# Fetching each expert buffer of the last six turns in two bounded halves, the second from a reversed copy of the table

## The reference

```python
s = jnp.einsum('thpd,hpkd->thpk', q, sub_keys)
sv, si = lax.top_k(s, PEER_TOPK)
cidx = (si[:, :, 0, :, None] * N_KEYS + si[:, :, 1, None, :]).reshape(PEER_BLOCK, PEER_HEADS, -1)
best, pos = lax.top_k(cand, PEER_TOPK)
eidx = jnp.take_along_axis(cidx, pos, axis=-1)
g = jax.nn.softmax(best, axis=-1)
act = jax.nn.gelu(jnp.einsum('thkd,td->thk', expert_u[eidx], xb))
return jnp.einsum('thk,thkd->td', g * act, expert_v[eidx])
```

## Time and profile before

| | us |
|---|---|
| median of 3 runs (1407.13 to 1409.46) | 1408.75 |
| the profiled execution's own time | 1413.65 |
| its span, first to last instruction | 1412.3 |
| POOL busy in the span | 296.5 |
| turn 10's first fetch is issued at | 1138.81 |

### The profile page before, as it was taken

One profiled execution on the slowest core, in us unless ns is written; L12 is line 12 of the kernel. 1 busy time (PEld: TensorE's weight loads), 2 busy tenths in 40 slices (PEclk: granted clock), 3 DMA queues, 4 the chain that ended last, 5 costly groups with the idle time before them and its releaser, 6 DMA issues.

```text
span 1412.3 us, 17514 instructions
## 1 busy us (share of the span) xinstructions
PE 1034.5 (73%) x6217; PEld 599.6 (42%) x6217; DVE 887.4 (63%) x2281; ACT 477.8 (34%) x1313; POOL 296.5 (21%) x265
## 2 busy tenths in 40 slices
PE   7998999999899999988878777754544454434444
PEld 4776655577665646434553432332222222202200
DVE  6488633448863536643347779586867776877664
ACT  2013523101353411455236655433323222332312
POOL 0000000000000000000023255533645444443441
PEclk9998999999899899998879899886666766656665
DMA  7452452445346142153059899999999999999997
GB/s 297 152 194 103 182 220 84 171 165 181 121 188 242 55 155 97 34 227 136 1 231 395 341 419 426 426 426 423 412 426 427 426 426 426 427 426 425 426 426 312
DMA packets 56105, 391.12 MB, mean 277 GB/s; under 512 B 9931, under 2 KB 13054, under 8 KB 15954
## 3 DMA queue, kind: packets, MB, share of 16 engines
q0 software_dynamic: 37440, 268.45, 45.5%
q1 hardware_dynamic: 18578, 121.56, 23.2%
HBM read 387.89 MB, written 1.05 MB: 275 GB/s over the span
## 4 chain that ended last, share of the span: by engine, by line
DVE 18%; PE 16%; DMA 14%; ACT 6%; issue 3%; another core or an unknown queue 3%; POOL 2%; ACTq 0%; DVEq 0%
PE bank L169 15%; DMA e_uv<-in_experts_dram,e_listed 14%; DVE e_uv L2791 6%; POOL e_uv L2988 2%; ACT e_diag L230 1%; ACT L230 1%; DVE e_hot L185 1%; DVE e_rest L2722 1%; ACT m_W L230 1%; PE bank L174 1%; DVE e_si L2720 1%; DVE e_si L2726 1%; DVE e_e L210 0%; DVE e_sv L2718 0%
## 5 line engine op out<-in xcount | busy, mean ns | idle before, releaser
L2988 POOL DMA_INDIRECT e_uv<-in_experts_dram,e_listed x252 | 286.8, 1138 | 1080.3 <-DVE e_listed L202 839.6
L169 PE MATMUL bank<-e_uv,e_diag 128*32 128x512 f32 x1024 | 231.3, 885 | 283.4 <-ACT e_diag L230 275.5
L2791 DVE CUSTOM_DVE_ANT_0 e_uv<-e_uv,e_h2q 128x1024 f32<-128x1024 f32 x192 | 229.4, 1224 | 83.1 <-DMA e_uv<-in_experts_dram,e_listed 79.0
L169 PEld LDWEIGHTS bank<-e_uv,e_diag 128*32 128x32 f32 x1024 | 41.3, 140 | 410.2 <-ACT e_diag L230 316.6
L169 PE MATMUL bank<-hT,weights 128*128 128x256 f32 x640 | 145.4, 388 | 2.4 <-DVE hT L191 1.4
L169 PEld LDWEIGHTS bank<-hT,weights 128*128 128x128 f32 x640 | 123.9, 195 | 21.8 <-DVE hT L191 1.6
L230 ACT ACT_TABLE_LOAD x81 | 103.9, 1283 | 7.9 <-PE bank L169 1.9
L169 PE MATMUL bank<-weights,hT 128*128 128x512 f32 (+1 forms) x256 | 101.5, 552 | 1.5 <-DVE hT L191 1.5
L197 DVE SCALAR_TENSOR_TENSOR conv<-ubuf,vec,conv 128x256 f32<-128x256 f32 x240 | 96.8, 479 | 0.6
L230 ACT ACTIVATE e_act<-e_dot 128x4 f32<-128x4 f32 (+1 forms) x81 | 16.6, 205 | 234.6 <-DVE e_dot L2791 212.4
L169 PE MATMUL bank<-weights,mixT 128*128 128x512 f32 x192 | 88.6, 616 | 2.3 <-DVE mixT L202 1.6
(11 more groups left out here) (383 smaller groups left out, 1419.0 us busy)
## 6 DMA issues: line engine op xcount, KB each, us to landing
weights<-in_ada_dram SPq DMA_DIRECT2D x8, 2048.0 KB, 8.3
weights<-in_layer_out_dram SPq DMA_DIRECT2D x6, 2048.0 KB, 8.1
e_w_pq<-in_w_pq_dram SPq DMA_DIRECT2D x12, 1024.0 KB
weights<-in_layer_cmp_dram SPq DMA_DIRECT2D x4, 2048.0 KB, 8.4
weights<-in_layer_q_dram SPq DMA_DIRECT2D x2, 2048.0 KB, 8.4
weights<-in_layer_kvc_dram SPq DMA_DIRECT2D x2, 2048.0 KB, 12.0
weights<-in_layer_gb_dram SPq DMA_DIRECT2D x2, 2048.0 KB, 15.1
weights<-in_layer_ga_dram SPq DMA_DIRECT2D x2, 2048.0 KB, 15.1
```

The costliest lines, as they stand in the source:

```text
L169: ins = self.engine.matmul(out, lhsT, rhs, start=start, stop=stop, **kw)
L2791: dve.mark(c.nc.vector.tensor_tensor_reduce(u, u, h2q[tt][n], 1.0, 0.0, MUL, ADD, m["dot"][:, j:j + 1]), ("dots_set", g, c0) if n == c1 - ...
L2988: ins = c.nc.gpsimd.indirect_dma_start(out=to, out_offset=None, in_=rows, in_offset=bass.IndirectOffsetOnAxis(ap=of, axis=0))
```

## The change

For batches 40 to 62 (turns 10 to 15 without the last batch) each buffer is now filled by two indirect DMAs. The first reads `experts` with the same list and a bound of 8191: rows whose number is larger are left out. The second reads `experts_back`, a second table in HBM that holds the same rows in reversed order, with the list 16383 - number, under the same bound, so that it fills exactly the partitions that the first left out. The second fetch of a buffer waits until the first has landed, and it is issued one batch later: after the first fetches of batch g come the second fetches of batch g-1. DVE writes the reversed list just before the list. The host lays out the second table outside of the measured time.

```diff
+IN_HALVES = range(10, len(TURNS))
+HALF_ROWS = N_KEYS * N_KEYS // 2
...
+        if k in IN_HALVES:
+            dve.ts(m["listed_back"][:, k % 2], spread, -1.0, MUL, float(N_KEYS * N_KEYS - 1), ADD)
         dve.copy(m["listed"][:, k % 2], spread, tell=("list_set", k))
...
+    def other_half(g):
+        for n in range(BATCH):
+            j, slot = PLACE[g] * BATCH + n, g % PER_TURN * BATCH + n
+            pool.wait_ge(*at(f"uv_in{j}", "half", g))
+            fetch(m["uv"][j], A["experts_back"], m["listed_back"][:, g // PER_TURN % 2, slot:slot + 1], f"uv_in{j}", g,
+                  bounds_check=HALF_ROWS - 1, oob_is_err=False)
 
     for g in range(BATCHES):
         if g % PER_TURN == 0:
             pool.wait_ge(*at("list_set", g // PER_TURN))
+        if g == BATCHES - 1:
+            other_half(g - 1)
...
-            if g < BATCHES - 1:
+            if g < BATCHES - 1 and g // PER_TURN in IN_HALVES:
+                fetch(m["uv"][j], A["experts"], m["listed"][:, g // PER_TURN % 2, slot:slot + 1], f"uv_in{j}", "half", g,
+                      bounds_check=HALF_ROWS - 1, oob_is_err=False)
+            elif g < BATCHES - 1:
                 fetch(m["uv"][j], A["experts"], m["listed"][:, g // PER_TURN % 2, slot:slot + 1], f"uv_in{j}", g)
...
+        if g < BATCHES - 1 and (g - 1) // PER_TURN in IN_HALVES:
+            other_half(g - 1)
```

More of the change, by code:

```diff
@@ L1571, in second_memory @@
             ("dot", [P, BUFS], F32), ("act", [P, BUFS], F32), ("spare", [P, 1], F32),
-            ("listed", [P, 2, BUFS], U32), ("listed_uv", [P, 2, BATCH], U32), ("weight", [P, 2, BUFS], F32), ("sv", [P, 2, TOPK], F32), ("si", [P, 2, TOPK], U32),
+            ("listed", [P, 2, BUFS], U32), ("listed_uv", [P, 2, BATCH], U32), ("listed_back", [P, 2, BUFS], U32), ("weight", [P, 2, BUFS], F32), ("sv", [P, 2, TOPK], F32), ("si", [P, 2, TOPK], U32),
             ("sif", [P, 2, TOPK], F32), ("best", [P, 2, TOPK], F32), ("pos", [P, TOPK], U32), ("part", [P, TOPK], U32),
@@ L2985, in peer_gpsimd, with fetch @@
     halves = A["experts"].rearrange("n (a d) -> (n a) d", a=2)
-    def fetch(to, rows, of, *tell):
-        ins = c.nc.gpsimd.indirect_dma_start(out=to, out_offset=None, in_=rows, in_offset=bass.IndirectOffsetOnAxis(ap=of, axis=0))
+    def fetch(to, rows, of, *tell, **kw):
+        ins = c.nc.gpsimd.indirect_dma_start(out=to, out_offset=None, in_=rows, in_offset=bass.IndirectOffsetOnAxis(ap=of, axis=0), **kw)
         c.events.tell(ins, *tell, by=16)
+    def other_half(g):
[4 more added lines that the diff above has]
+                  bounds_check=HALF_ROWS - 1, oob_is_err=False)
     for g in range(BATCHES):
@@ L3127 @@
     keys = inputs["sub_keys_2"][0].transpose(0, 3, 1, 2).reshape(PEER_H, P, 2 * N_KEYS)
-    laid = [("constants", constants()[0]), ("experts", rows), *weights_laid(inputs), ("w_pq", w_pq), ("keys", keys)]
+    laid = [("constants", constants()[0]), ("experts", rows), ("experts_back", rows[::-1]), *weights_laid(inputs), ("w_pq", w_pq), ("keys", keys)]
     arrays = {name: np.ascontiguousarray(a) for name, a in laid + [(n, inputs[n]) for n in _USED]}
```

## The result

The changed kernel takes 1462.53 us (median of 4 runs, 1450.23 to 1466.91); the kernel before took 1409.11 in the same comparison (4 runs). The ratio is 1.0359, 95% interval 1.0326 to 1.0392: 53 us slower, where the forecast had 20. The profiled execution took 1460.39 us, with a span of 1459.1.

What follows compares the result with a forecast made beforehand. The DMA stream bounds the kernel before; with 32 fetches a turn POOL would. From 1158 us, 228 + 22 + 9 + 3 gives the last issue at 1420 and the end at 1431.7, some 20 us slower: 1429 us, range 1409 to 1484.

Steps and rivals of the forecast that it cites:

- rival 1: POOL is the bound at its present price, 1417 to 1450 us; the forecast itself, 52%.
- 1.24 us a fetch: POOL's step for a fetch without a wait: 0.94 us plus 0.30 us until the next.
- the 184 fetches: Fetches POOL has left from 1158 us on, 192 - 8; at 1.24 us each, 228.2 us.
- the stand until 1158: POOL stands 9 us at batch 40's second fetch, until the first half of buffer 4 lands at 1158.
- the register move: Instruction on POOL ahead of each bounded fetch: taken as 0.05 us each, 9 us in all.
- The other waits of POOL, with a short queue: POOL's waits for lists and freed buffers are met unless routing on DVE comes between; 3 us for all turns.
- Slow fetches: POOL's fetches that start inside a train of back-to-back dots take longer: 22 us, between 17 and 34.
- The second: Rival: the bounded fetch costs POOL more; +0.25 us each gives 1475, +0.5 us 1521; 22%.
- the third: Rival: not slower, as leaving out rows spares POOL their descriptors; 1407 to 1411 us; 12%.
- the sixth: Rival: faster, as reading from half of the table speeds up the stream; 3%.
- the fourth: Rival: left-out rows cost the DMA engines; read in full 1634 us, at a fifth 1454 or more; 8%.
- The fifth: Rival: single dots block POOL's fetches too, 1.05 us each, 80 us in 5.75 turns, 1509 us; 3%.

Runs made afterwards that it cites:

- e8_quarters: e3_columns with quarter rows, as many fetches and half the bytes: 1457.82 us, ratio 1.0288 to the kernel before.
- e1_again: The changed kernel once more, unedited: 1464.98 us, ratio 1.0350 to the kernel before.
- e13_early: The kernel before with 192 empty fetches (all rows left out) on POOL ahead of the expert stream: 1642.98 us, ratio 1.1617.
- e16_paused: e13_early with POOL waiting after every fourth empty fetch for its completion: 1562.72 us, ratio 1.1102 to the kernel before.
- e15_fills: The kernel before with two 128x512 fills on POOL in place of each of the 92 second fetches: 1418.19 us, ratio 1.0030.
- e17_fill_behind: The changed kernel with one 128x512 fill on POOL behind each second fetch: 1481.30 us, ratio 1.0546 to the kernel before.
- e12_short_dots: The changed kernel with dots over 512 of 1024 columns in turns 10 to 15: 1468.96 us, ratio 1.0411 to the kernel before.
- e6_bound_only: The kernel before with a bound that leaves nothing out on the fetches of batches 40 to 62: 1413.98 us, ratio 0.9982.
- e2_empty92: The kernel before with 92 fetches that leave out every row at the second fetches' places, nobody waiting for them: 1456.62 us, ratio 1.0278.
- e3_columns: The kernel before with each of the 92 buffers fetched as a u half and a v half, no bound, no wait: 1458.07 us, ratio 1.0308.
- e5_three_turns: The changed kernel with halves in the last three turns only, 44 fetches added: 1438.83 us, ratio 1.0173 to the kernel before.
- e11_shift128: The kernel before with an unused tile of 128 B per partition ahead of the buffers: 1418.78 us, ratio 1.0051.
- e2_empty46: The kernel before with 46 empty fetches, two behind each batch, 24 issues a turn: 1424.14 us, ratio 1.0093.

## Why the prediction was right or wrong

**Right in its question and its answer.** POOL has become the bound (rival 1): e8_quarters takes as long with half of the bytes. Its 1.24 us a fetch, the 184 fetches, the stand until 1158 (1157.04), the bounded fetch with what loads its bound (9 us in all, though on POOL's row and not in the gap) and the end (12.4 us behind the last fetch, 11.5 forecast) all measured as forecast. The bytes are equal, and so are the packets of 8 KB and more (69,355 - 29,202 = 40,153 against 40,151). That the bounded fetch costs the forecast 9 us is luck: the price stands in its own row, where the forecast had none, and not in the gap before it, where it had 9 for the register move. GB/s fell to 291 to 397, lower than the 390 to 410 forecast, by the waits. One reading of the earlier trace rows was off without consequence: nine tenths and 412 GB/s or more begin with slice 24, and the last slice moves 312.

**The step that failed** is "The other waits of POOL, with a short queue ... I allow 3 us for all turns": they took 28 us in the profiled execution. (In e1_again, as long in all, they took 8; there the term for slow fetches, 22 us forecast and 35 measured, and a later start of turn 10 make up the rest.) I had worked out that list and buffers come in time (6.8 of 11 us, 10.8 of 22 us) with each engine at its own pace of before, "unless routing on DVE comes between". What came between was the routing, late because PE was slowed by POOL's own issuing. A margin taken from durations of before held no longer, since before POOL never issued for longer than its bursts. That issuing without a pause holds up the other engines, and how far this goes, is shown by e13_early and e16_paused; that occupation without issues does not, by e15_fills; that POOL can give most of its waits away, by e17_fill_behind. That the routing of turn 12 was late for this reason is read from the timeline, where PE and ACT run without pauses again only after POOL's train has ended.

**Slow fetches**: 22 forecast, 26 in the profiled execution, 32 to 40 in most of the others. The size was near, but what makes them was read wrongly, by me before the result and in the experiments: it isn't the train of dots. A fetch is slow when it starts while a dot is running, single or not, and it is longer by what is left of that dot, less 0.12 us. A dot that stood alone in the changed kernel, and one in the kernel before, each with the fetch that started inside it:

```profile
1299.73 1.23 DVE L2795 CUSTOM_DVE_ANT_0 e_uv<-e_uv,e_h2q 128x1024 f32<-128x1024 f32 x1 [0.87 <-DMA e_uv<-in_experts_back_dram,e_listed_back]
1300.08 1.74 POOL L2992 DMA_INDIRECT e_uv<-in_experts_dram,e_listed  x1 [0.30 <-issue]
...
1180.41 1.23 DVE L2791 CUSTOM_DVE_ANT_0 e_uv<-e_uv,e_hT 128x1024 f32<-128x1024 f32 x1 [0.92 <-DMA e_uv<-in_experts_dram,e_listed]
1181.00 1.44 POOL L2988 DMA_INDIRECT e_uv<-in_experts_dram,e_listed  x1 [0.30 <-issue]
```

The first dot has 0.88 us left at 1300.08, less 0.12 is 0.76, and the fetch takes 0.75 us more than 0.99. From 1138 us on, 62 fetches of the changed kernel start inside a dot. All 42 with more than 0.25 us of it left are slow, each by this sum within 0.02 us; of the 129 others two are slow (1.21 and 1.16 us). A train only adds that a fetch in the last 0.03 us of a dot meets the next one in full. The fetch at 1182.75, which the forecast took as proof that a single dot does no harm, had started 0.09 us before the dot. With shorter dots less is left to meet, hence the 8 us of e12_short_dots; but making these fetches cheap bought nothing.

**The rivals.** The second (a dearer bounded fetch) is refuted by 0.99 us and by e6_bound_only; the third and the sixth by the time; the fourth (left-out rows cost the DMA engines) by e2_empty92 and e3_columns, which leave out everything and nothing and cost the same. The fifth (single dots block too) has the mechanism right and the price wrong: it took 1.05 us for every dot, 80 us in all, where only the fetches that start inside a dot pay, and only for its rest, 26 us. The Trainium skill says in "SBUF — State Buffer" (SBUF: two separate sides) that of a VectorE instruction with two inputs in SBUF and a GpSimd instruction that reads SBUF, the one that starts first has the shared ports for its whole length and the other is blocked. The trace agrees for the fetches; it doesn't for the dots, since those that started beside a running fetch took their usual 1.22 us. The forecast's reading of the skill, that every overlap would block, left out who starts first.

**What stays open**: what inside the chip holds the other engines up. The rows only show them idle without a semaphore. The Trainium skill says in "Runtime: NRT & Kernel Launch" (Instruction fetch mechanics) that engines are refilled with instructions in blocks of 16 KiB (256 instructions) over a DMA queue of their own and that this is mostly hidden. The page of the profile agrees with the first (queue q8: 49 packets, 0.80 MB, so 16 KB each). On the second, the trace of e13_early speaks against blocks that land late: q8 is PE's by its count (49 x 256 = 12,544, and PE has 12,434 matmuls and weight loads); its packets go out at 518 us and then at 634, at about the same places of PE's program as those of 517 and 551 us in the kernel before. PE's pace breaks at 547.5, 30 us behind the first, and it doesn't come back with the second. So late instructions are a guess from PE's timeline, and a block that is missing in this queue is not what the trace shows. Open too is how the 53 us of the changed kernel divide between slow fetches and pauses: whichever I took away, the other grew. e5_three_turns lost 28 us with hardly a stretch of PE.

No experiment beat the kernel before.

## What to carry to other kernels

Count the issues of indirect DMAs on POOL per turn of the stream: 16 and 24 in 42 us are free, 32 are not, and splitting a fetch doubles them whatever it moves. Each costs 1.24 to 1.29 us, and up to 1.04 us more if it starts while DVE is in a dot. When an engine goes from bursts to issuing without a break, don't take the other engines' durations and margins from the trace of before: look for waits on "issue" in them, and leave short pauses. Pauses of the other engines matter only once POOL is the bound. Compare GB/s in the stretches that the change does not touch; a different number there is a cause of its own, such as the address at which a buffer begins.

## What the runs showed of the hardware that was not expected

- Indirect fetches issued by POOL every 1.30 us without a pause bring all other engines nearly to a stop after some 30 us: PE at one matmul in 2.8 us, ACT once idle for 69 us and DVE for 34 us with nothing to wait for, with the DMA engines at 2%. A wait after every fourth fetch (1.9 to 6.5 us) is enough to prevent it.
- An indirect fetch that starts while DVE is in a dot over 1024 columns is longer by what is left of the dot, less 0.12 us (42 of 42 with more than 0.25 us left in the changed kernel); one that starts before the dot is not, and neither is the dot.
- Adding 92 fetches that leave out all their rows costs as much as splitting 92 fetches in two (+41 and +43 us).
- A left-out row of an otherwise used fetch is a packet of its own (11,776 in the changed kernel). A fetch that leaves out all its rows has 32 packets and not 144 (40,384 on the queue of e2_empty92, 2,944 more than before).
- Buffers that start 128 B further on take 8 KB rows at 419 to 422 GB/s (e11_shift128) and 4 B further on at 413 to 421 (e2_empty46) in full slices, instead of 425 to 427; 256 B further on nothing changes. The 128 B alone were 0.5% of the kernel's time.
